# Long convolution: the signal's transform issued one pass ahead, the spectra's product in a work space of its own, and the filter butterflies ahead of the next filter tiles

## The reference, cut to what matters

```
def long_conv(u, k_f, skip):
    L = u.shape[1]
    uf = _f32(u)
    y = jnp.fft.irfft(jnp.fft.rfft(uf, n=2 * L, axis=1) * k_f, n=2 * L, axis=1)[:, :L]
    return (y + uf * _f32(skip)).astype(u.dtype)
...
    k_f = hyena_filters(L, f_w1, f_b1, f_w2, f_b2, f_w3, f_b3, freq)
    z = parts[0]
    for o in range(HY_ORDER):
        z = parts[o + 1] * long_conv(z, k_f[:, o], skip[o])
```

## Time and profile before

| | before |
|---|---|
| median of 3 runs | 5146.45 us (5143.6 to 5149.0) |
| profiled execution | 5143.57 us |
| its span, first to last instruction | 5141.9 us |
| mean granted TensorE clock | 0.923 |
| busy over the span | PE 4357.6 us, DVE 1922.3, ACT 1159.5, POOL 278.6 |
| the stage, first to last instruction | 1937.1 to 2533.4 us, some 596 us |

### The profile page before, as it was taken

The page is one execution under the profiler, slowest core; times in us unless marked ns, Lnnn a source line. Parts: engine busy times, 40 slices in busy tenths (PEclk is TensorE's granted clock), DMA queues, the critical chain, the costliest instruction groups (busy, mean ns, idle before and its releaser), DMA issues. The chain is left out here.

```text
span 5141.9 us, 52299 instructions
## 1 busy us (share of the span) xinstructions
PE 4357.6 (85%) x17971; PEld 2236.7 (43%) x17971; DVE 1922.3 (37%) x2999; ACT 1159.5 (23%) x1920; POOL 278.6 (5%) x390
## 2 busy tenths in 40 slices
PE   3699799997799997999589978859999599779995
PEld 1354455554344445777444445423333244333332
DVE  1233444443222104998546647221111423411113
ACT  0122354442111012222020336101111244111111
POOL 0100000000000000111000000000000200000001
PEclk7899899998899997999799989979999799989998
DMA  6322221113344412111231120447653511266745
GB/s 246 112 64 74 53 49 36 35 35 120 153 153 171 185 56 77 51 51 50 98 108 60 46 78 21 152 170 291 233 210 136 183 42 41 94 259 235 277 183 207
DMA packets 262066, 629.15 MB, mean 122 GB/s; under 512 B 74045, under 2 KB 153997, under 8 KB 242489
## 3 DMA queue, kind: packets, MB, share of 16 engines
q1 hardware_dynamic: 219314, 497.53, 27.7%
q0 software_dynamic: 21856, 102.40, 5.3%
q10 hardware_dynamic: 20776, 27.64, 1.5%
HBM read 899.85 MB, written 117.73 MB: 198 GB/s over the span
## 5 line engine op out<-in xcount | busy, mean ns | idle before, releaser
L3348 PE MATMUL blocks_h<-moe_w,blocks_xT 128*64 128x512 f32 x3072 | 689.1, 602 | 35.6 <-ACT blocks_xT L3290 15.6
L3348 PEld LDWEIGHTS blocks_h<-moe_w,blocks_xT 128*64 128x64 f32 x3072 | 222.4, 139 | 458.1 <-issue 453.2
L1611 PE MATMUL hyp_acc<-hy_hT,hyp_weights 128*128 128x512 f32 x768 | 337.8, 599 | 27.6 <-DMA hyp_weights<-in_hy_w_in 27.6
L3369 PE MATMUL blocks_acc<-moe_w,blocks_hidT 128*64 128x512 f32 x1536 | 340.1, 595 | 1.6 <-DVE blocks_hidT L3253 1.6
L969 PE MATMUL att_scores<-att_kT,att_qT 64*128 64x512 f32 (+3 forms) x768 | 252.2, 549 | 20.9 <-DMA att_v<-scratch_V 20.9
L700 PE MATMUL lat_acc<-lat_w_in,lat_hT 128*128 128x512 f32 (+1 forms) x640 | 244.2, 537 | 4.2 <-DMA lat_w_in<-in_attn_w_in 4.2
L2151 PE MATMUL evp_acc<-ev_hT,evp_weights 128*128 128x512 f32 x512 | 227.5, 606 | 10.5 <-DMA evp_weights<-in_ev_in_w 4.6
L1611 PEld LDWEIGHTS hyp_acc<-hy_hT,hyp_weights 128*128 128x128 f32 x768 | 146.3, 193 | 204.3 <-issue 204.3
L905 DVE TENSOR_REDUCE att_nmax<-att_scores 128x1 f32<-128x1280 f32 x128 | 190.2, 1486 | 101.6 <-PE att_scores L969 101.6
L993 PE MATMUL att_turn<-ident,att_probs 128*128 128x128 f32 x1280 | 192.9, 281 | 41.5 <-DVE att_o L935 22.6
L873 ACT ACTIVATE att_probs<-att_scores,att_nmax 128x1280 f32<-128x1280 f32 x128 | 169.9, 1327 | 173.9 <-DVE att_nmax L905 171.9
(11 more groups left out here) (520 smaller groups left out, 5931.8 us busy)
## 6 DMA issues: line engine op xcount, KB each, us to landing
moe_w<-in_ex_w SPq DMA_DIRECT2D x288, 2048.0 KB
hyp_m_weights<-in_mod_w POOLq DMA_DIRECT2D x6, 8192.0 KB, 24.1
mod_weights<-in_ada_w SPq DMA_DIRECT2D x6, 4096.0 KB, 23.2
scratch_y_rows<-blocks_y ACTq DMA_DIRECT2D x48, 512.0 KB, 8.5
hyp_weights<-in_hy_w_in SPq DMA_DIRECT2D x8, 2048.0 KB, 27.4
scratch_parts<-hyp_uT SPq DMA_DIRECT2D x24, 512.0 KB, 3.3
evp_weights<-in_ev_in_w SPq DMA_DIRECT2D x5, 2048.0 KB, 12.7
lat_w_in<-in_attn_w_in SPq DMA_DIRECT2D x4, 2048.0 KB, 19.3
```

Of the source, the lines that this page charges most:

```text
L1611: mm = nc.tensor.matmul(acc[:, m % 2, half * NC:(half + 1) * NC], weights[:, ws, kt, c:c + P], hT[:, kt, half * NC:(half + 1) * NC], start ...
L3348: mm = nc.tensor.matmul(out[mine, :], xT[:, s, kt, mine], w[:, l, kt, :], start=(kt == 0), stop=(kt == KT - 1))
L3369: mm = nc.tensor.matmul(acc[mine, c, :], hidT[:, kt, mine], w2[:, l, kt, c * NC:(c + 1) * NC], start=(kt == 0), stop=(kt == FT - 1))
```

## The change

Six things, all in `stage_long_conv`:
1. TensorE's pass i no longer transforms the signal of pass i but, after `k_transform(i + 1)`, that of pass i+1 (`u_transform`). The first signal is transformed in the prologue, between `k_transform(0)` and `filters(1)`. ScalarE's copies follow the same order.
2. The copies into `xu` wait until VectorE has read the tile of the pass before (`xu_read`); their wait for `z_made` is gone.
3. VectorE's product takes only its first two operations from `xu`; the rest goes through a new buffer `work`. It waits for all of the filter's spectrum at its start, and before each `ft` for the `z` of the one before.
4. `ktmp` is no buffer of its own any more but half of `tmp`.
5. `k_butterfly(i + 1, ft)` moves from the inverse's loop (before r=2 and r=3) to a place directly behind the product and ahead of `filters(i + 2)`.
6. The skip weights are loaded by pass, one row of 256 at a time, on SP's queue (`load_skip`), rather than once.

```diff
--- before.py
+++ after.py
@@ -1671,7 +1671,7 @@
         negt = sb("negt", [P, TILES])
-        deltas, skip = sb("deltas", [P, CCH]), sb("skip", [1, PASSES * CCH])
+        deltas, skip = sb("deltas", [P, CCH]), sb("skip", [1, CCH])
         ones = sb("ones", [P, P])
@@ -1679,7 +1679,8 @@
         xu, xk = sb("xu", [P, MT, PH, 2, CCH]), sb("xk", [P, MT, PH, 2, CCH])
-        tmp, ktmp = sb("tmp", [P, PH, 2, CCH]), sb("ktmp", [P, 2, 2, CCH])
+        tmp, work = sb("tmp", [P, PH, 2, CCH]), sb("work", [P, PH, 2, CCH])
+        ktmp = tmp[:, 0:2, :, :]
         vk = sb("vk", [P, MT, PH, 2, CCH])
@@ -1694,7 +1695,7 @@
                              "extra_made", "tapped"))
-        sized = sem("sized")
+        sized, skip_in, xu_read = sem("sized"), sem("skip_in"), sem("xu_read")
         u_steps, k_steps, vk_ready, z_made, y_made = (
@@ -1702,7 +1703,7 @@
         COPIES = 2 * MT
-        U_STEPS = 7
+        U_STEPS = 6
         FIX = 2
@@ -1747,6 +1748,10 @@
                     sp.dma_start(tiled(u), tokens(i)).then_inc(u_in, 16)
+
+                def load_skip(j):
+                    sp.wait_ge(tapped, signals(j))
+                    sp.dma_start(skip[:, :], skips[:, bass.ds(j * CCH, CCH)]).then_inc(skip_in, 16)
@@ -1756,15 +1761,18 @@
                 sp.dma_start(negt[:, :], d["k_negt"]).then_inc(w3_in, 16)
-                sp.dma_start(skip[:, :], skips).then_inc(w3_in, 16)
+                load_skip(0)
                 sp.dma_start(fwd[:, :, :, :, :], d["k_fwd"]).then_inc(mats_in, 16)
...
                 sp.dma_start(inv[:, :, :, :, :], d["k_inv"]).then_inc(mats_in, 16)
+                load_skip(1)
...
                         load_u(i + 1)
+                    if ahead:
+                        load_skip(i + 2)
                     sp.wait_ge(conv_done, signals(i * PH + PH))
@@ -1780,7 +1788,7 @@
                             if not isinstance(j, int) or j:
-                                pe.wait_ge(x_copied[b], signals(j * COPIES - MT))
+                                pe.wait_ge(x_copied[b], signals(j * COPIES))
                         else:
@@ -1820,6 +1828,10 @@
+                def u_transform(j):
+                    pe.wait_ge(u_in, signals(j * 16 + 16))
+                    transform(u_parts, lambda ft: u_copied(j, ft) - 1, u_made)
+
                 def norm(j):
@@ -1832,16 +1844,15 @@
                     k_transform(0)
+                    u_transform(0)
                     filters(1, range(NF))
...
                         pe.wait_ge(filt_ready, signals(i * NF + 2 * NF))
-                    pe.wait_ge(u_in, signals(i * 16 + 16))
-                    transform(u_parts, lambda ft: u_copied(i, ft) - 1, u_made)
-                    if more:
                         k_transform(i + 1)
+                        u_transform(i + 1)
                     if ahead:
@@ -1878,6 +1889,8 @@
                     for ft in range(MT):
+                        if made is u_made and not (isinstance(n, int) and n == 0):
+                            act.wait_ge(xu_read, signals(n * MT + (ft + 1 - MT)))
                         for b in range(PH):
@@ -1888,12 +1901,13 @@
                     load_deltas(0)
-                    act.wait_ge(w3_in, signals(16 * 11))
+                    act.wait_ge(w3_in, signals(16 * 10))
                     decays(0)
...
                     k_copies(0)
+                    copies(0, u_made, xu)
                     decays(1)
@@ -1901,10 +1915,9 @@
                         load_deltas(i + 2)
-                    act.wait_ge(z_made, signals(i * MT))
-                    copies(i, u_made, xu)
                     if more:
                         k_copies(i + 1)
+                        copies(i + 1, u_made, xu)
                     if ahead:
@@ -1944,7 +1957,8 @@
                     dve.wait_ge(tapped, signals(j))
-                    tt(extra[:, :], n_bank[0:1, 0:CCH], skip[:, bass.ds(j * CCH, CCH)], ALU.mult).then_inc(extra_made, 1)
+                    dve.wait_ge(skip_in, signals(j * 16 + 16))
+                    tt(extra[:, :], n_bank[0:1, 0:CCH], skip[:, :], ALU.mult).then_inc(extra_made, 1)
                     dve.wait_ge(extra_made, signals(j + 1))
@@ -1972,7 +1986,7 @@
-                    dve.wait_ge(w3_in, signals(16 * 11))
+                    dve.wait_ge(w3_in, signals(16 * 10))
                     fw, bw = w3[:, :, 0, :], w3[:, :, 1, :]
@@ -1993,25 +2007,30 @@
                         link = Chain(dve, u_steps, i * (MT * U_STEPS) + ft * U_STEPS).link
-                        x, k = xu[:, ft, :, :, :], vk[:, ft, :, :, :]
+                        x, k, w = xu[:, ft, :, :, :], vk[:, ft, :, :, :], work[:, :, :, :]
                         dve.wait_ge(x_copied[PH - 1], signals(u_copied(i, ft)))
+                        dve.wait_ge(vk_ready, signals(i * MT + MT))
+                        dve.wait_ge(z_made, signals(i * MT + ft))
                         tt(tmp[:, 0:2, :, :], x[:, 0:2, :, :], x[:, 2:4, :, :], ALU.add)
-                        link(tt(tmp[:, 2:4, :, :], x[:, 0:2, :, :], x[:, 2:4, :, :], ALU.subtract))
-                        link(turn(nc.vector, tmp[:, 0, :, :], tmp[:, 1, :, :], tmp[:, 2, :, :], tmp[:, 3, :, :], x, 1))
-
-                        dve.wait_ge(vk_ready, signals(i * MT + (ft + 1)))
-                        link(tt(tmp[:, :, :, :], x, k, ALU.mult))
-                        tt(x[:, :, 0, :], x[:, :, 0, :], k[:, :, 1, :], ALU.mult)
-                        link(tt(x[:, :, 1, :], x[:, :, 1, :], k[:, :, 0, :], ALU.mult))
+                        tt(tmp[:, 2:4, :, :], x[:, 0:2, :, :], x[:, 2:4, :, :], ALU.subtract).then_inc(xu_read, 1)
+                        dve.wait_ge(xu_read, signals(i * MT + (ft + 1)))
+                        link(turn(nc.vector, tmp[:, 0, :, :], tmp[:, 1, :, :], tmp[:, 2, :, :], tmp[:, 3, :, :], w, 1))
+
+                        link(tt(tmp[:, :, :, :], w, k, ALU.mult))
+                        tt(w[:, :, 0, :], w[:, :, 0, :], k[:, :, 1, :], ALU.mult)
+                        link(tt(w[:, :, 1, :], w[:, :, 1, :], k[:, :, 0, :], ALU.mult))
                         link(tt(tmp[:, :, 0, :], tmp[:, :, 0, :], tmp[:, :, 1, :], ALU.subtract))
-                        link(tt(tmp[:, :, 1, :], x[:, :, 0, :], x[:, :, 1, :], ALU.add))
-
-                        tt(x[:, 0:2, :, :], tmp[:, 0:2, :, :], tmp[:, 2:4, :, :], ALU.add)
-                        link(tt(x[:, 2:4, :, :], tmp[:, 0:2, :, :], tmp[:, 2:4, :, :], ALU.subtract))
+                        link(tt(tmp[:, :, 1, :], w[:, :, 0, :], w[:, :, 1, :], ALU.add))
+
+                        tt(w[:, 0:2, :, :], tmp[:, 0:2, :, :], tmp[:, 2:4, :, :], ALU.add)
+                        link(tt(w[:, 2:4, :, :], tmp[:, 0:2, :, :], tmp[:, 2:4, :, :], ALU.subtract))
                         dve.wait_ge(y_made, signals(i * PH))
-                        turn(nc.vector, x[:, 0, :, :], x[:, 1, :, :], x[:, 2, :, :], x[:, 3, :, :], z[:, ft, :, :, :], 3)\
+                        turn(nc.vector, w[:, 0, :, :], w[:, 1, :, :], w[:, 2, :, :], w[:, 3, :, :], z[:, ft, :, :, :], 3)\
                             .then_inc(z_made, 1)
+                    if more:
+                        for ft in range(MT):
+                            k_butterfly(i + 1, ft)
                     if ahead:
@@ -2019,8 +2038,6 @@
                             totals(i + 2, range((r - 1) * PH // 2, r * PH // 2))
-                        if more and r >= PH - MT:
-                            k_butterfly(i + 1, r - (PH - MT))
                         if ahead and r == PH - 1:
...
                         dve.wait_ge(y_made, signals(i * PH + (r + 1)))
```

## The result

The changed kernel takes 5177.76 us (median of 5 runs, 5175.5 to 5184.3) against 5146.45 us: the ratio is 1.0061 with a 95% interval of 1.0046 to 1.0076. It is slower by 31 us, beyond the end of the forecast range (5168). The forecast had slower at 0.47 and no change at 0.45, so the direction is little to its credit, and its size was a third of what came.

A forecast was written before the change was run, and what follows sets the result against it. It took a chain hopping between TensorE and VectorE as the bound. Prologue +3.8, six passes +9.8 and tail -4.1 summed to +9.5 us, giving 5156.0 us against the 5146.45 median; range 5139 to 5168.

The forecast's parts named there:

- The chain that bounds the kernel before: Looped pass: product 34.77, hop 0.21, TensorE 22.41, first half of the signal's transform with copy 7.74; sum 65.13 us.
- The product's start at 3.45 us: VectorE's next product starts 3.45 us after TensorE ends r=3: 3.2 us of VectorE's tail plus 0.25 of branch.
- The butterflies on the path: Between VectorE's product and its filter tiles: two butterflies of 3.86 us and 0.1 for the product's completion, 7.85 us.
- the idle of 5.9 us before the filters: TensorE, behind r=0, stands from 41.9 to 47.8 us until VectorE's first filter tile leaves its bank.
- The loop's branch: VectorE's branch back to the loop's head: 0.25 us visible, from ScalarE's row; bounds 0 and 1.6 us.
- Prologue and tail: Before the loop the first product comes 3.8 us later; pass 6, with no filters ahead, gets 4.1 us shorter.
- The DMAs at nothing: Per-pass skip loads and the signal's load on SP's queue stay hidden and cost 0 us.
- Rival C: VectorE's filters come free right behind the product, so butterflies don't reach TensorE: 61 us a pass, 5119 us; chance 0.08.
- step 5: Clock falls behind the new idle: second half of the filters takes 5.5 us, then r=1 to r=3 13.8 as before.
- Rival D: Costlier hand-overs: branch shows its full 1.6 us, or every pass loses 3.15 us of clock; about 5164 us; chance 0.13.
- Rival B: The clock outlives the 5.9 us idle before the second filters: passes of 65.05 us, 5139.6 us in all; chance 0.07.

The follow-up runs named there:

- the kernel with the butterflies back: The changed kernel with the filter butterflies put back among the inverse's phases: 5138.13 us, ratio 0.9978 to the kernel before, 63.7 us a pass.
- filler: The changed kernel with 12 more unused full-size products directly behind the inverse r=0: 5149.34 us, ratio 1.0000 to the kernel before, 65.4 us a pass.
- idle kept, full products behind: The changed kernel with an explicit wait for the first filter tile, then 8 unused 128-row products ahead of the second filters: 5183.32 us, ratio 1.0065.

## Why the prediction was wrong

**Right.** The chain that bounds the kernel before. The product's start at 3.45 us (3.50). The butterflies on the path: 7.85 us from the product's end to the first filter tile (2136.03 to 2144.01 = 7.98), and the idle of 5.9 us before the filters (5.86). The loop's branch, taken by ScalarE's row: VectorE stands 0.25 us there (0.25 forecast). For the wait that the Trainium skill's rule on taken branches gives (Runtime: NRT & Kernel Launch, Instruction fetch mechanics) the prediction had a bound of 1.6 us; no wait longer than 0.3 us shows. Whether the loop's head lay outside the fetched pages, which that rule asks for, no run tells. Prologue and tail within 0.8 us. The DMAs at nothing: no instruction of the pass waits for one. Rival C, that the butterflies' time would not reach TensorE, was false of the changed kernel; the kernel with the butterflies back does what it describes, in about 62 us a pass where the clock holds and 61 were worked out. It gained 11 us (ratio 0.9978) where 27 were worked out, some 9 us less by the clock lost behind the tap's wait in three passes.

**Wrong: step 5,** "With it the clock falls again: the second half of the filters takes 3.44 + 2.05 = 5.5 us". The mechanism was right and the term was mis-sized: 2.05 us were carried over from an idle with inverse products of 128 rows behind it to one with filter products of 65 rows behind it. There the loss is 3.55 us in the filters, since they never get the clock back, and another 0.9 to 2.4 us in r=1 and r=2, in which it comes back. Over the six passes it is 4.65, 5.49, 5.90, 4.44, 5.38 and 5.86, mean 5.29 us. With it the pass is 67.1 - 2.05 + 5.29 = 70.34, against 70.57 measured, the six give +29.3, and the sum of the prediction becomes +29 us against +29.6 in the stage. Rival D took the worst row's 3.15 us as the bound, for the same reason too low.

The bound was there to be read. In the trace of the kernel before, the stage's first filters stand behind a long idle; the stretch from their first to their last product (columns as in rows 1):

```profile
1952.58:1966.60 14.02, 14.02 (x16) 5.22 (x16) 5.65 (x10) 2.11 (x2) 0.00 (x0) 0.50 0.70 289
```

Sixteen instructions, 14.02 us without a gap, and the clock is 0.50 throughout. A price for filters behind an idle was on this row, and I took the one of another kind of product. A second one was among the rows read the earlier trace rows: eight filter instructions behind 2.82 us of idle are listed with 6.06 us, where the eight before them took 3.60, a loss of 2.5 us behind an idle half as long as the one forecast. Rival B used the start of that row, at the full clock, and not its length.

**Shown and not shown.** Shown by experiments: that the butterflies' place costs the loss (undone, and done alone), that 5.2 us a pass are clock (filler), that behind the same idle other products lose less (idle kept, full products behind), that the loss is halved when the filters' products are padded to 128 rows and stays when they are split in columns. Open: how many rows it takes between 65 and 128, and whether it is the row count as such or something that goes with it; not tried. Open too: whether narrow products help the clock to fall.

## What to carry to other kernels

Work moved ahead on one engine delays all that is queued behind it there. Ask which of that the other engine waits for, not whether the moved work has its own data early. And when TensorE's idle moves, price the lost clock by the products that will run behind the new place, from a row with the same products behind an idle; if there is choice, put products that fill the array behind an idle, and the narrow ones behind these. Where a short idle of TensorE can't be removed, useless products of full size in it can be cheaper than the clock that it costs.

## What the runs showed of the hardware

- Products of 65 rows did not bring the clock back from 1.2 to 2.4 GHz: 14.0 us of them at the stage's start, 7.0 us in each pass of the changed kernel. The same products with 63 rows of zeros added did, within the 6.2 us that eight of them took, and cost no time by themselves (3.44 us for eight at the full clock either way). The Trainium skill (TensorE: Matmul & The Clock Gate, Part 1) tells of sustained matmul activity as what releases the clock; by that alone, TensorE busy without a gap, the 14 us row could not be. The measurement decides.
- The clock can fall while TensorE is busy: after 2.4 us of idle it fell 0.6 us into the narrow products in the pass shown. With 128 rows it held in three of five passes; that the narrow products helped it to fall is suggested only.
- A wait of 3.15 us in the same place of a loop cost 2.9 us of clock in three passes and nothing in two others. A small idle's price varies from pass to pass, and only a mean over passes shows it.
